# Projecting input rows before their norm factors are known, with the first weights on a second queue

## What is computed

```python
h = jnp.concatenate([filler, meta, x], axis=1)
u = rms_norm(h, pre_mix_gain[l])      # row * rsqrt(mean(row^2) + 1e-6) * gain
proj = u @ w_in[l]                    # 1024 -> qa, ka, va, qb, kb, vb, g
qa = rope(qa.reshape(B, Lp, SWA_Q_HEADS, HEAD_DIM), pos)
ka = rope(ka.reshape(B, Lp, SWA_KV_HEADS, HEAD_DIM), pos)
va = va.reshape(B, Lp, SWA_KV_HEADS, HEAD_DIM)
...
gates = jax.nn.sigmoid(g + b_gate[l])
```

## Time and profile before

| | |
|---|---|
| median of 3 runs | 978.37 us (978.27 to 979.35) |
| the profiled execution's own time | 978.03 us |
| its span, first to last instruction | 976.2 us |
| TensorE busy | 949.0 us (97%) |
| VectorE, ScalarE, GpSimd busy | 685.8, 533.3, 126.4 us |

### The profile page before, as it was taken

The page is one execution under the profiler, slowest core; times in us unless marked ns, Lnnn a source line. Parts: engine busy times, 40 slices in busy tenths (PEclk is TensorE's granted clock), DMA queues, the critical chain, the costliest instruction groups (busy, mean ns, idle before and its releaser), DMA issues.

```text
span 976.2 us, 15556 instructions
## 1 busy us (share of the span) xinstructions
PE 949.0 (97%) x6212; PEld 846.6 (87%) x6212; DVE 685.8 (70%) x1251; ACT 533.3 (55%) x1019; POOL 126.4 (13%) x145
## 2 busy tenths in 40 slices
PE   8999999999999999999999999799899999999997
PEld 7999888999999988888988898698699898888885
DVE  6888776777478676766667679776665577676765
ACT  7876666765456643434355877444444364434443
POOL 2211111211032000000001139610100000000001
PEclk9999999999999999999999999999999999999999
DMA  9543334334377556565647642201353446656541
GB/s 319 188 135 131 130 112 148 99 120 134 126 260 236 174 174 215 173 216 173 204 141 247 224 165 88 87 1 44 131 172 130 151 132 210 199 170 200 171 169 43
DMA packets 115863, 154.71 MB, mean 158 GB/s; under 512 B 2728, under 2 KB 98224, under 8 KB 115536
## 3 DMA queue, kind: packets, MB, share of 16 engines
q1 hardware_dynamic: 113376, 142.91, 44.4%
q0 software_dynamic: 1952, 10.42, 3.0%
q10 hardware_dynamic: 464, 0.40, 0.2%
HBM read 150.56 MB, written 3.16 MB: 157 GB/s over the span
## 4 chain that ended last, share of the span: by engine, by line
PE 84%; DVE 8%; ACT 5%; issue 2%; DMA 0%; POOL 0%; POOLq 0%; DVEq 0%; ACTq 0%
PE ps L820 14%; PE ps L796 8%; PE ps L798 8%; PE ps L797 8%; PE ps L821 7%; PE ps L1107 4%; PE ps L1080 4%; PE ps L1081 4%; PE ps L1082 4%; PE ps L839 3%; PE ps L841 3%; PE ps L840 3%; PE ps L782 3%; DVE wlo L1338 2%; PE ps L809 2%; PE ps L811 2%
## 5 line engine op out<-in xcount | busy, mean ns | idle before, releaser
L1338 DVE TENSOR_TENSOR wlo<-raw,whi 128x1024 fp32r<-128x1024 f32 (+1 forms) x268 | 326.8, 1237 | 161.2 <-ACT whi L1962 160.9
L1962 ACT ACTIVATE whi<-raw 128x1024 fp32r<-128x1024 f32 (+1 forms) x268 | 274.2, 1051 | 132.8 <-PE ps L821 53.8
L820 PE MATMUL ps<-R1b,whi 128*128 128x512 f32 x576 | 201.8, 393 | 0.0
L796 PE MATMUL ps<-R1b,whi 128*128 128x256 f32 (+1 forms) x592 | 172.6, 291 | 0.8 <-DVE wlo L1338 0.8
L798 PE MATMUL ps<-R1b,wlo 128*128 128x256 f32 (+1 forms) x592 | 167.7, 283 | 0.0
L797 PE MATMUL ps<-R1b,whi 128*128 128x256 f32 (+1 forms) x592 | 167.6, 283 | 0.0
L821 PE MATMUL ps<-R1b,wlo 128*128 128x256 f32 x576 | 161.4, 280 | 0.0
L820 PEld LDWEIGHTS ps<-R1b,whi 128*128 128x128 f32 x576 | 108.1, 188 | 24.7 <-issue 0.5
L796 PEld LDWEIGHTS ps<-R1b,whi 128*128 128x128 f32 x592 | 111.5, 188 | 10.1 <-issue 7.9
L798 PEld LDWEIGHTS ps<-R1b,wlo 128*128 128x128 f32 x592 | 111.8, 189 | 0.0
L797 PEld LDWEIGHTS ps<-R1b,whi 128*128 128x128 f32 x592 | 111.5, 188 | 0.2
(11 more groups left out here) (294 smaller groups left out, 1801.3 us busy)
## 6 DMA issues: line engine op xcount, KB each, us to landing
raw<-in_w_in SPq DMA_DIRECT2D x34, 1024.0 KB, 5.0
raw<-in_w_ffn_in SPq DMA_DIRECT2D x22, 1024.0 KB, 5.1
raw<-in_w_ffn_out SPq DMA_DIRECT2D x11, 1024.0 KB, 5.5
raw<-in_w_gate SPq DMA_DIRECT2D x11, 1024.0 KB, 5.4
raw<-in_w_up SPq DMA_DIRECT2D x11, 1024.0 KB, 5.3
raw<-in_w_down SPq DMA_DIRECT2D x11, 1024.0 KB, 5.6
raw<-in_w_out SPq DMA_DIRECT2D x8, 1024.0 KB, 5.1
raw<-in_w_xkv SPq DMA_DIRECT2D x8, 1024.0 KB, 5.4
```

The source lines that it names most:

```text
L796: e.matmul(o, hi[:, kt, c], R[0][:, kt, 0:n], start=kt == 0, stop=False)
L820: e.matmul(B[:, :].rearrange("p (a n) -> p a n", a=2), hi[:, kt, c], R[2][:, :, kt, 0:256], start=kt == 0, stop=False)
L1338: e.tensor_tensor(half_of(wlo[i % HL], i, k), half_of(raw[i % RAW], i, k), f32(half_of(whi[i % HL], i, k)), SUB).then_inc(lo_split(i, (i, k)))
L1962: return e.activation(o, i, f, **kw)
```

## The change

The input comes from HBM already transposed (`x_cols`, arranged by the host from `x` and the meta tokens, with the gain in the first 8 columns), in two transfers on SyncE's queue. ScalarE and VectorE make `R1` from it with the gain alone (`xsplit`). Unit 0 is loaded in two halves, which ScalarE's queue issues, while SyncE's queue carries the columns and then units 1 and 2. The rows `X`, the meta tokens, the identity matrix, the rope tables and the parameters come after unit 2 and ahead of unit 3. The row factors are computed from `X` (`rowstat`), spread over the partitions by three matmuls (`rowtab`), multiplied into the rope tables in place, and kept as a table for the gates. The values are multiplied by them in the copy behind their transposes. The gates get a multiplication by VectorE, and their Tanh follows as a step of its own (`tanh`). `ropek` takes its matmuls in the order high by high, high by low, low by high, and waits for each part separately. The transposes of the input go.

In the plan the first four rope steps are no longer taken behind their products. The products of the two query blocks and the two key blocks wait in four PSUM banks of the pool `head`, until `rowtab`, which stands behind the first half of unit 2.

```diff
     def opening():
+
+        def laid(k, key, b):
+            step("roped", key, b, k)
+            step("rotate", key, b, k)
+
         order.append(("w_in", "featk", 0, 256))
         for j in range(2):
             take(0, j)
             step("ropek", j, 0)
-            if j:
-                for b in range(2):
-                    step("roped", "qa", b, b)
-                    step("rotate", "qa", b, b)
-                state["rope"] = 2
             yield 1
-
-    def values(key, col0, u):
+        order.append(("w_in", "feat", 1024, 256))
+        for j in range(2):
+            take(1, j)
+            step("ropep", "ka0", j, j, 1, 2 + j)
+            if j == 0:
+                step("rowstat")
+            yield 1
+        state["rope"] = 4
+        for j, _ in enumerate(values("va", 1280, 0, ("setup",))):
+            if j == 0:
+                step("rowtab")
+                laid(0, "qa", 0)
+                laid(1, "qa", 1)
+            else:
+                laid(2, "ka0", 0)
+                laid(3, "ka0", 1)
+                step("swap")
+            yield 1
+
+    def values(key, col0, u, *then):
 
         order.append(("w_in", "feat", col0 + 256 * u, 256))
         i = len(order) - 1
...
             step("v", key, u, j, i)
             if j:
                 step("vt", key, u, 0)
+            else:
+                for s in then:
+                    step(*s)
             yield 1
 
     def behind(work, *steps):
...
         yield from work
...
     def gates(u):
-        return unit(("gate", u), "w_in", "feat", 4608 + 256 * u)
+        yield from unit(("gate", u), "w_in", "feat", 4608 + 256 * u)
+        step("tanh", u)
...
-    step("rows", "n1")
+    step("xsplit", 0, 4)
     ahead(1)
-    step("turn", "n1", (0, 2))
-    ahead(2)
-    step("turn", "n1", (4, 6))
-    step("turnm")
+    step("xsplit", 4, 8)
...
-    va = behind(values("va", 1280, 0), ("swap",), ("setup",))
-    units = [opening(), rope("ka0", 1024, 0), va, qa[1], ga[0], qa[2], ga[1], qa[3], ga[2], qb[0], vb[0], kb[0],
+    units = [opening(), qa[1], ga[0], qa[2], ga[1], qa[3], ga[2], qb[0], vb[0], kb[0],
...
+        xcols = F[:, 0:8 + 8 * NT]
+        xT = xcols[:, 8:].rearrange("p (k n) -> p k n", k=8)
...
+        row0 = stat("row0", 9)
+        rs0 = row0[:, 6:9]
+        rsb0 = par("lam", 0, 256)
...
+            def rowtab():
+                B = claim("head", ("row0",), (norm_dve, "tables"))
+                p.wait_ge(id_in, 0)
+                p.wait_ge(norm_pool, "row0")
+                for i in range(2):
+                    mm(B[:, 128 * i:128 * i + 128], rs0[:, i:i + 1].to_broadcast([128, 128]), ident)
+                mm(B[:, 256:NT], rs0[0:16, 2:3].to_broadcast([16, 128]), ident[0:16, 0:16]).then_inc(norm_pe("row0"))
...
-                B = claim("gemm", ("rope", k), (rope_act, k), (rope_dve, ("cos", k)))
-                if n > NR:
-                    p.wait_ge(norm_dve, ("n1", "lo", 8))
+                B = claim("head" if k < 4 else "gemm", ("rope", k), (rope_act, k), (rope_dve, ("cos", k)))
...
+                        claim("head", ("rope", k), (rope_act, k), (rope_dve, ("cos", k)))
+                p.wait_ge(hi_split, (i, part))
+                for w, r in ((hi, 0), (hi, 1), (lo, 0)):
+                    if w is lo:
+                        p.wait_ge(lo_split, (i, part))
+                    for kt in range(4 * part, 4 * part + 4):
+                        if r:
+                            p.wait_ge(norm_dve, ("n1", "lo", kt))
+                        elif w is hi:
+                            p.wait_ge(norm_act, ("n1", "hi", kt))
+                        for k in range(2):
+                            m = e.matmul(ps("rope", k)[:, 0:256], w[:, kt, 128 * k:128 * k + 128], R1[r][:, kt, 0:256],
+                                         start=kt == 0 and r == 0 and w is hi, stop=kt == 7 and w is lo)
...
-            keep(banks[7].t, 13, half[:, 0:1].to_broadcast([128, 128]), half[:, 0:1].to_broadcast([128, 256]))
+            keep(banks[7].t, 12, half[:, 0:1].to_broadcast([128, 128]), half[:, 0:1].to_broadcast([128, 256]))
...
+            def xsplit(first, end):
+                for kt in range(first, end):
+                    d.wait_ge(norm_act, ("n1", "hi", kt))
+                    stt(R1[1][:, kt, :], xT[:, kt, :], xcols[:, kt:kt + 1], f32(R1[0][:, kt, :]), MUL, SUB).then_inc(
+                        norm_dve(("n1", "lo", kt)))
+
+            def rowstat():
+                d.wait_ge(x1_in, 0)
+                ttr(sq0[1], X[:, 1, :], X[:, 1, :], 1.0, 0.0, MUL, ADD, row0[:, 1:2]).then_inc(norm_dve("sq0"))
+                d.wait_ge(norm_dve, "sq0")
+                d.wait_ge(norm_act, "sq0")
+                ts(row0[:, 3:6], row0[:, 0:3], 1.0 / 1024, 1e-6, MUL, ADD).then_inc(norm_dve("ms0"))
+
+            def rowtab():
+                B = ps("row0")
+                d.wait_ge(norm_pe, "row0")
+                d.wait_ge(ca_in, 0)
+                for name in ("cos", "sin"):
+                    e.tensor_tensor(caf(name), caf(name), B[:, 0:NT], MUL).then_inc(norm_dve("tables"))
+                d.wait_ge(set_act, "lam")
+                e.tensor_copy(rsb0, B[:, 0:256]).then_inc(norm_dve("tables"))
...
             def rotate(key, b, k):
                 n = ROPE[key][1]
                 a, c = turned[k % 3]
-                d.wait_ge(ca_in, 0)
+                d.wait_ge(norm_dve, "tables")
...
-                e.tensor_copy(VAL[key][:, 0:2, c], B[:, 0:256].rearrange("p (t n) -> p t n", t=2)).then_inc(val_dve((key, u, j)))
+                d.wait_ge(norm_pool, "row0")
+                e.tensor_tensor(VAL[key][:, 0:2, c], B[:, 0:256].rearrange("p (t n) -> p t n", t=2),
...
+            def gate(u, j, i):
+                if j:
+                    d.wait_ge(gemm, ("gate", u))
+                    d.wait_ge(norm_dve, "tables")
+                    e.tensor_tensor(GA[:, 2 * u:2 * u + 2, :], ps("gate", u)[:, :].rearrange("p (b n) -> p b n", b=2), rep(rsb0, 2),
+                                    MUL).then_inc(gate_dve(u))
...
+            e.memset(row0, 0.0).then_inc(set_dve("row0"))
...
             def split(i, k):
-                a.wait_ge(raw_in[i % RAW], i)
+                a.wait_ge(*((first_in, 0) if (i, k) == (0, 0) else (raw_in[i % RAW], i)))
                 if i >= HL:
                     a.wait_ge(gemm, ("half", i - HL, k) if alike(order, i) else ("unit", i - HL))
                 act(half_of(whi[i % HL], i, k), half_of(raw[i % RAW], i, k)).then_inc(hi_split((i, k)))
...
+            def xsplit(first, end):
+                a.wait_ge(xb_in if first else xa_in, 0)
+                for kt in range(first, end):
+                    act(R1[0][:, kt, :], xT[:, kt, :], scale=xcols[:, kt:kt + 1]).then_inc(norm_act(("n1", "hi", kt)))
+
+            def rowstat():
+                a.wait_ge(set_dve, "row0")
+                for signal_, v_, m, i in ((x_in, X[:, 0, :], 128, 0), (meta_in, metat, 16, 2)):
+                    a.wait_ge(signal_, 0)
+                    act(sq0[i][0:m], v_, ACT.Square, accum_out=row0[0:m, i:i + 1]).then_inc(norm_act("sq0"))
...
+            def tanh(u):
+                a.wait_ge(gate_dve, u)
+                a.wait_ge(set_dve, "hb")
+                for k in range(2):
+                    act(GA[:, 2 * u + k, :], GA[:, 2 * u + k, :], ACT.Tanh, bias=hb[:, 2 * u + k:2 * u + k + 1],
+                        scale=0.5).then_inc(gate_act(u))
...
-            e.dma_start(metat, A["meta_tokens"]).then_inc(meta_in(0), 16)
-            e.dma_start(ca[:, 0:128], A["const_a"][:, 0:128]).then_inc(id_in(0), 16)
-            e.dma_start(pc[:, 0:8], A["params"][:, 0:8]).then_inc(mix_in(0), 16)
...
+            src, k, n = unit_src(0)
+            dst = raw[0][:, 0:k * n].rearrange("p (k n) -> p k n", k=k)
+            e.dma_start(dst[:, 0:4, :], src[:, 0:4, :]).then_inc(first_in(0), 16)
+            e.dma_start(dst[:, 4:8, :], src[:, 4:8, :]).then_inc(raw_in[0](0), 16)
...
+            def rowstat():
+                pool.wait_ge(norm_dve, "ms0")
+                power(rs0, row0[:, 3:6]).then_inc(norm_pool("row0"))
...
-            e.dma_start(X[:, 0, :], x_src[:, 0, :]).then_inc(x_in(0), 16)
-            e.dma_start(X[:, 1, :], x_src[:, 1, :]).then_inc(x1_in(0), 16)
+            cut = 8 + 4 * NT
+            e.dma_start(xcols[:, 0:cut], A["x_cols"][:, 0:cut]).then_inc(xa_in(0), 16)
             for i in range(len(order)):
                 src, k, n = unit_src(i)
+                dst = raw[i % RAW][:, 0:k * n].rearrange("p (k n) -> p k n", k=k)
+                if i == 0:
+                    e.dma_start(xcols[:, cut:], A["x_cols"][:, cut:]).then_inc(xb_in(0), 16)
+                    continue
                 if i >= RAW:
                     s.wait_ge(lo_split, i - RAW)
-                e.dma_start(raw[i % RAW][:, 0:k * n].rearrange("p (k n) -> p k n", k=k), src).then_inc(raw_in[i % RAW](i), 16)
-                if i == 0:
```

(12 more changed lines are left out.)

76 lines of the change are left out of this document (20 added, 56 removed).

## The result

The changed kernel takes 987.12 us (median of 4 runs, 986.87 to 988.97), beside 978.32 for the kernel before in the same measurement: a ratio of 1.010, interval 1.0088 to 1.0113. That is 8.8 us slower, where 4.7 were forecast, and outside the range. The profiled execution took 986.87 us.

What follows compares the result with a forecast made beforehand. TensorE, busy 949.0 of 976.2 us, was taken to bound the kernel, with its first scores waiting for the swap. 978.03 + 3.5 (late scores) + 1.5 (clock) + 0 (gates) = 983.0 us, range 979.5 to 985.5.

Steps and rivals of the forecast that it cites:

- What bounds it: Whole kernel: TensorE is busy 949.0 of 976.2 us, so a shift at about 35 us shifts the end as much.
- The earlier start: Opening: first product at 9.3 us, unit 1 at 15.2 instead of 19.31, 4.1 us won but swallowed by the swap's wait.
- When unit 3 lands: Weight loading in the opening: 6.98 MB moved instead of 6.14, so unit 3 lands at 22.7 us instead of 20.4.
- The third case (unit 3 in time): Rival, opening: second queue adds bandwidth, products bind the chain, scores at 36.4, 979.3 to 980.8 us; chance 0.12.
- From there to the scores: From unit 3's landing (T) to the swap's end: T + 15.95 = 38.65 us, scores 3.5 us late.
- Clock: Behind the wait at the first scores: TensorE at reduced clock loses 1.5 us, bounds 0 to 3.
- Gates and values: Eight gate multiplications on VectorE, 0.69 us each, and value copies turned multiplications: cost 0, bounds 0 and 2.0 us.
- Sum: Whole kernel: 978.03 + 3.5 (scores) + 1.5 (clock) = 983.0 us.
- The early start: Rival, opening to end: TensorE never waits for the swap, 3.6 us won, 974.4 us; chance 0.08.

Runs made afterwards that it cites:

- e1: Changed kernel with identity, rope tables and parameters loaded behind unit 3 instead of ahead of it; 988.11 us.
- e6: Changed kernel with both halves of unit 0 issued by SyncE's queue between the two parts of the columns, instead of by ScalarE's queue; 988.69 us.
- e5: Changed kernel with twelve matmuls on a constant ahead of the first scores, run while TensorE waits for the swap; 988.74 us.
- e13: Changed kernel with Tanh straight from PSUM (gates lack row factors) and an equal-size VectorE multiplication into an unread place for each gate but the last; 984.86 us.
- e11: Changed kernel with gates copied from PSUM by ScalarE and multiplied by GpSimd, each Tanh of gates 0 to 6 behind the next half unit; 988.01 us.
- e15: Changed kernel with rows, identity and cosine/sine tables ahead of unit 2, row sums before its splits, early copies and rotations, parameters last, gates unchanged; 984.17 us, ratio 1.0071.

## Why the prediction was wrong in size

**What bounds it** held: TensorE's busy time is unchanged, and the 5.0 us won at unit 1 are lost to the stall ahead of the first scores, 2.04 us at the transposes and 7.04 for the swap.

**The earlier start.** Forecast 9.3 and 15.2, measured 7.84 and 14.28. The step that failed is "I take it that they share by packets rather than by bytes": the first half of unit 0 landed at about 5.9 us and not at 8.2, and was split from 6.36 on. What then set the first product was the end of `keep`, which the prediction has at 7.7, well ahead of its 9.3. It had no weight, as said, since the wait swallowed it.

**When unit 3 lands.** Forecast 22.7, measured 23.80, 1.1 us of the miss. The step is the count of bytes, that with 6.98 MB moved unit 3 is there: the DMA page of the first 24 us has 7.86 MB.

```profile
DMA packets 5936, 7.86 MB, mean 327 GB/s; under 512 B 224, under 2 KB 5151, under 8 KB 5935
```

The rate was as taken (355 and 363 GB/s in 12 to 24 us, beside the earlier trace rows), so some 0.8 MB of what was issued behind unit 3 had moved by 23.8, ahead of its last piece. Those would be 2.2 us, and the miss is half of that. The kernel before had moved 6.37 MB by 20.4, where 6.14 were counted, so 0.2 MB of it were in the forecast's 20.4 already; and the first 6 us moved 0.16 MB more than before (238 GB/s against 212). What is left, 0.4 MB, is 1.1 us. e1 bears out the rest of the step: bytes taken from ahead of unit 3 gave back their time, up to the scores. In the other five kernels with this opening the splits start at 24.18 to 24.58. The Trainium skill (DMA: Bandwidth & Descriptors, Issuing engines are not separate DMA queues) has all issuers on the same 16 DMA engines; e6 agrees, with unit 3 at 23.77 from one queue and 23.80 from two (18.86 and 19.11 us behind the first columns). The third case (unit 3 in time) falls with it.

**From there to the scores.** Forecast T + 15.95, measured T + 16.7. The step is "VectorE is free for it": instead of done at T + 11.4, VectorE ended the value products at T + 11.9 (the low split took 1.57 instead of 1.2), then had to rotate the third block, and its sine of the fourth took 0.87 us beside GpSimd's addition. 0.75 us. The chain's other pieces were within 0.3 of their rows.

**Clock.** 1.5 forecast, 1.9 measured, inside the bounds 0 to 3. One stretch of 10.2 us at half rate, from 35.3 to 45.5, half of it behind the wait's end. That it can be added to the other terms was wrong: e5 took it away and ended no earlier.

**Gates and values.** This is the step that failed outright: "I take 0; the bounds are 0 and 2.0, these waits doubled". It is 3.0. I looked at VectorE's busy share and at TensorE's waits, and not at what Tanh's wait would do to ScalarE's order. Of the 3.0, the four waits for ScalarE in front of scores make up 1.4 (2.0 to 3.4, which the bound had), and waits at L994, which before did not exist, 1.0. Most of the last 0.6 is in the two stretches between scores that hold these new waits: TensorE is also busy for 12.74 and 12.73 us in them, where it was for 12.48 and 12.47 before, at full clock in both; why, no run shows. Even the bound looked only at waits that were already there. What the runs show in place of the 0: the gates cost 3 us, by where Tanh stands in ScalarE's order, and not by VectorE's time (e13, e11).

**Sum.** Scores +1.9 more than forecast, clock +0.4, gates +3.0, 0.2 on the way to the FFN, less 1.7 for the half-clock stretch that was missing late in this execution: 5.0 + 3.8 = 8.8, and the spans differ by 8.9. The 1.7 are luck: with as many late stretches as the kernel before, the miss would have been 5.5 and not 3.8.

**Rivals.** The early start did not come through in any kernel. Its condition, the swap's end by 31.5, was not met even in e15, where the swap ended at 34.8.

## What to carry to other kernels

Before moving work off the start, list in order what each engine does from the last landing to the first point where TensorE needs it; that list, not the first product, sets the gain. When an operation gets a new producer on another engine, look at what stands ahead of that producer in its queue and what stands behind the waiting instruction on its own: a busy share of 75% hid a cost of 3 us for eight operations of 0.7 us. And a stall is cover: taking it or its clock loss away shows the next engine's backlog, so remedies don't add up. Before a gain of half a microsecond is read from one trace each, see how far the start of executions with the same opening differs; here it was 0.6 us at the first columns and 0.8 at the first scores.
